# Router on the raw residual, joint placement of both choices, first item by a zero-one product, gate inside the expert results

## The chip, the cores and the metric

The kernel runs on one core of a Trainium2 chip. A core has five engines that run their own instruction streams and meet at semaphores: TensorE (PE, matmuls; weight loads are shown apart as PEld), VectorE (DVE), ScalarE (ACT), GpSimd (POOL) and SyncE (SP, which here only starts transfers). Sixteen DMA engines move data between HBM and the on-chip memory; SP, ACT and POOL each own a queue to them. TensorE's clock has two levels, 2.4 GHz and 1.2 GHz; the profile gives the granted clock of a stretch as 1.00 or 0.50. The metric is the device time of one execution in microseconds (us), the median of several. All data is float32.

## The reference, cut to what matters

Two blocks run one after the other on 512 tokens of 1024 features. The first has two layers of attention, the second one layer of windowed attention beside a convolution, and then the part that this change is about, a mixture of experts:

```python
h2 = rms_norm(x, g_norm2) * (1.0 + sc2) + sh2
x  = x + gt2 * hier_moe(h2, ...)
return rms_norm(x, g_final)

def hier_moe(h, ...):
    g_logits = h @ w_rg + b_rg                       # 4 groups
    grp      = argmax(g_logits)
    e_logits = (h @ w_re + b_re)[token, grp]         # 8 experts of that group
    top_val, top_idx = top_k(e_logits, 2)
    top_w = softmax(top_val) * softmax(g_logits)[grp]
    # each (token, choice) is given to its expert; out = sum of top_w * expert(h)
    expert(x) = (silu(x @ w_gate[e]) * (x @ w_up[e])) @ w_down[e]   # 1024 -> 512 -> 1024
```

There are 32 experts, so 1024 (token, choice) pairs in all. `sc2`, `sh2` and `gt2` are rows of 1024 that come from a condition vector.

## The kernel before

The program is one block of instructions per engine, written out by hand; no scheduler orders it. What sets the order on an engine is the order of the code, and what sets it between engines are semaphores. Tokens lie in four tiles of 128 (`TT = 4`), features in eight blocks of 128 (`KT = 8`). PE writes into eight banks: four that ACT empties (`act_banks`), two for transposes (`tr_banks`, ACT too) and two that DVE empties (`dve_banks`). `claim` takes the next bank of a set and waits until it was freed.

**Before the experts.** `project_out("wout2", ...)` multiplies the mixed rows by the output weights in two halves of four token tiles. DVE adds each half to the residual `x` (`residual_part`, lines 1519 and 1522). When both halves of a tile are in, ACT squares it (line 926), POOL turns the sum into 1/rms in six small instructions (`rstd`, lines 1231 to 1241), DVE scales the tile into `C_tok` (`scale_tile`, line 1429), PE transposes it (`norm_tile`, line 489) and ACT applies scale and shift on the way into `hT` (line 934). Then PE makes the 36 router logits of each tile with 128 tokens stationary and 36 columns moving (line 796).

**Routing.** DVE (`route`) adds the bias (line 1344), picks the group and the two experts (`first_of`, to line 1363), and PE counts how many tokens before each one chose the same expert, by ten products with a matrix of ones and four with a triangular one (lines 805 and 807). DVE then works out the places of the first and of the second choice one after the other (lines 1367 to 1399), which gives `dest`. Each expert owns 96 rows (`SLOTS`); tokens beyond them go to further items.

**Rows and items.** POOL scatters the normed rows from `C_tok` to `expert_rows` in HBM with eight indirect transfers (line 1276), waits for all, and loads 96 rows for the first item and 96 for the second (`load_rows`, line 1281). An item is one expert on 96 rows, in a wide part of 64 and a narrow part of 32: PE transposes its rows (`flip_rows`, line 821), DVE scales and shifts them (`flip`, lines 1861 and 1864), PE multiplies by gate and up weights (`gate_up`, line 831), ACT and DVE make the SwiGLU, PE transposes (lines 855, 860) and multiplies by the down weights (`down`, line 838), ACT copies both results out (lines 1183 and 1185) and issues six stores (line 1190). SP loads the 6 MB of weights of item n+2 into the places that item n frees. 35 items run, the last three for tokens beyond 96 rows.

**Tail.** POOL gathers two result rows for each token, tile by tile (line 1304). Per tile ACT weighs the first (line 1209), DVE adds the weighted second (1901), multiplies by the gate `norm_row` (1902) and adds to `x` (1903), ACT squares (1217). After all four tiles POOL makes four 1/rms columns at once, DVE multiplies four tiles by them and the final gain (line 1908), and SP stores them.

**Two earlier places.** In the second layer's input products DVE forms the modulation rows and runs the 31 taps of the convolution (line 1779), and in front of the first layer's rotary part it forms the columns `mods[3]` and `aff[3]` (scale and shift of the rows for the experts).

## Time and profile before

| | us |
|---|---|
| median of 3 runs | 1803.24 |
| lowest, highest | 1801.92, 1804.38 |
| the profiled execution | 1801.39 |
| its span, first to last instruction | 1799.7 |
| PE busy | 1618.8 (90%) |
| DVE, ACT, POOL busy | 667.6 (37%), 423.0 (24%), 95.9 (5%) |
| mean share of the DMA engines over the span | 391.49 MB, 218 GB/s |

PE is busy nearly everywhere, so the places to read are those where it is not. The page's row of forty slices shows them: the first slice, the slices 24 and 25 (1080 to 1170 us, five tenths busy), and the last one. The first stretch is routing, the last one the tail. Between them stand the experts with PE at nine tenths and the DMA engines at nine tenths too. The chain that ended last is 79% PE, 12% DVE and 4% DMA.

### The profile page before, as it was taken

To read this page: it belongs to the slowest core of one execution; us is meant where nothing else is said; L and a number is where in the kernel's file an instruction comes from. 1 tells how busy PE (TensorE), PEld (TensorE's weight loads), DVE (VectorE), ACT (ScalarE), POOL (GpSimd) and SP (SyncE) were. 2 spreads that over 40 slices of the span, in tenths; PEclk is the share of its full clock that TensorE was granted. 3 is DMA by queue.
4 is the path that set the end of the run, shared out by engine and by line. 5 is a ranking of instruction groups with operands and counts; after the bars stand their busy time and mean duration, and the time that the engine had idled before them with its cause. 6 is when DMAs were issued, how large, how long until landed. Compare 5 with 4: busy or idle time off the path is not lost.

```text
span 1799.7 us, 23161 instructions
## 1 busy us (share of the span) xinstructions
PE 1618.8 (90%) x8968; PEld 810.9 (45%) x8968; DVE 667.6 (37%) x1203; ACT 423.0 (24%) x935; POOL 95.9 (5%) x223
## 2 busy tenths in 40 slices
PE   2999999789899999989998995599999999999990
PEld 2444445554455446546445645244444444444440
DVE  5664006972564133236995424111111111111114
ACT  2433005641201434232005422011111111111112
POOL 3000000111000000020000010200000000000002
PEclk9999999999999999999998995799999999999995
DMA  9653137800675310034220015599999999999974
GB/s 346 227 187 113 47 140 234 275 30 19 221 238 177 140 48 1 13 139 152 94 94 1 1 63 229 202 392 383 403 407 400 409 402 407 404 399 410 398 308 149
DMA packets 112007, 391.49 MB, mean 218 GB/s; under 512 B 11303, under 2 KB 20184, under 8 KB 102600
## 3 DMA queue, kind: packets, MB, share of 16 engines
q1 hardware_dynamic: 84960, 324.02, 47.0%
q0 software_dynamic: 12368, 44.96, 7.7%
q10 hardware_dynamic: 14616, 21.67, 3.4%
q8 instruction: 40, 0.66, 0.1%
q14 instruction: 23, 0.19, 0.0%
HBM read 348.54 MB, written 42.07 MB: 217 GB/s over the span
## 4 chain that ended last, share of the span: by engine, by line
PE 79%; DVE 12%; DMA 4%; ACT 2%; issue 2%; POOL 1%; ACTq 0%; DVEq 0%; SPq 0%; POOLq 0%
PE score_banks L831 20%; PE bank L513 13%; PE bank L838 10%; PE score_banks L505 10%; PE score_banks L513 8%; DVE bufD L1779 4%; PE bank L489 4%; PE score_banks L821 2%; PE bank L724 2%; PE score_banks L660 2%; PE score_banks L717 1%; PE bank L664 1%; DMA slots<-in_w_exp_up 1%; DVE bufD L1444 1%; DMA slots<-in_ada_w 1%
## 5 line engine op out<-in xcount | busy, mean ns | idle before, releaser
L831 PE MATMUL score_banks<-slots,hT 128*32 128x256 f32 (+1 forms) x3360 | 375.5, 453 | 3.7 <-DVE hT L1864 2.3
L831 PEld LDWEIGHTS score_banks<-slots,hT 128*32 128x32 f32 (+1 forms) x3360 | 148.0, 119 | 229.0 <-issue 187.0
L505 PE MATMUL score_banks<-hT,slots 128*128 128x512 f32 (+1 forms) x480 | 201.0, 577 | 11.1 <-ACTq L938 6.1
L838 PE MATMUL bank<-slots,hT 128*32 128x256 f32 (+1 forms) x1680 | 193.1, 454 | 0.0
L513 PE MATMUL score_banks<-slots,hT 128*128 128x512 f32 (+1 forms) x448 | 186.2, 575 | 0.9 <-PE score_banks L505 0.3
L513 PE MATMUL bank<-slots,hT 128*128 128x512 f32 x384 | 167.0, 594 | 2.7 <-ACTq L1007 1.5
L1870 DVE TENSOR_TENSOR mix<-probsT,score_banks 128x256 f32<-128x256 f32 x35 | 14.8, 422 | 382.4 <-ACT probsT L1171 382.4
L505 PEld LDWEIGHTS score_banks<-hT,slots 128*128 128x128 f32 x480 | 93.0, 196 | 113.5 <-issue 104.2
L513 PEld LDWEIGHTS score_banks<-slots,hT 128*128 128x128 f32 x448 | 86.3, 198 | 93.7 <-issue 93.7
L838 PEld LDWEIGHTS bank<-slots,hT 128*32 128x32 f32 (+1 forms) x1680 | 69.9, 118 | 111.4 <-issue 88.4
L513 PEld LDWEIGHTS bank<-slots,hT 128*128 128x128 f32 x384 | 72.2, 190 | 93.5 <-issue 91.5
L1779 DVE SCALAR_TENSOR_TENSOR bufD<-bufC,col,bufD 128x512 f32<-128x512 f32 x120 | 80.5, 748 | 0.5 <-DVE norm_row L1494 0.3
L1171 ACT ACTIVATE probsT<-score_banks 128x256 f32<-128x256 f32 x35 | 13.4, 384 | 276.6 <-PE score_banks L831 276.6
L1444 DVE SCALAR_TENSOR_TENSOR bufD<-slots,silu_c,bufD 128x512 f32<-128x512 f32 x98 | 73.7, 752 | 4.2 <-DVE bufD L1444 0.5
L513 PE MATMUL bank<-slots 128*128 128x512 f32 x160 | 69.7, 593 | 1.3 <-ACTq L1007 1.0
L821 PE MATMUL score_banks<-k_sb,bufD 96*128 96x96 f32 x288 | 37.4, 274 | 30.3 <-DMA bufD<-expert_rows 30.3
L1628 DVE TENSOR_REDUCE negmax<-score_banks 128x2 f32<-128x1024 f32 x32 | 39.0, 1222 | 61.0 <-PE score_banks L660 60.2
L1519 DVE TENSOR_TENSOR mix<-bank,gate_row 128x512 f32<-128x512 f32 x24 | 16.6, 692 | 117.4 <-PE bank L513 117.3
L1444 DVE SCALAR_TENSOR_TENSOR slots<-slots,silu_c 128x512 f32<-128x512 f32 x70 | 52.6, 752 | 11.3 <-DMA slots<-in_w_mod 4.5
L1861 DVE TENSOR_TENSOR hT<-score_banks,aff 128x384 f32<-128x384 f32 x72 | 36.8, 553 | 42.9 <-PE score_banks L821 42.9
L505 PE MATMUL score_banks<-slots 128*128 128x512 f32 x104 | 46.9, 611 | 3.9 <-ACTq L1094 3.3
L1872 DVE TENSOR_TENSOR mix<-probsT,score_banks 128x128 f32<-128x128 f32 x35 | 10.0, 286 | 105.1 <-ACT probsT L1173 105.1
(269 smaller groups left out, 1640.0 us busy)
## 6 DMA issues: line engine op xcount, KB each, us to landing
slots<-in_w_exp_gate SPq DMA_DIRECT2D x35, 2048.0 KB, 16.7
slots<-in_w_exp_up SPq DMA_DIRECT2D x35, 2048.0 KB, 21.4
slots<-in_w_exp_down SPq DMA_DIRECT2D x35, 2048.0 KB, 22.2
slots<-in_w_in SPq DMA_DIRECT2D x16, 2048.0 KB, 8.2
slots<-in_w_mod SPq DMA_DIRECT2D x24, 1024.0 KB, 5.3
slots<-in_ada_w SPq DMA_DIRECT2D x18, 1024.0 KB, 7.3
expert_rows<-norm_row POOLq DMA_DIRECT2D x1, 16896.0 KB, 62.5
bufD<-expert_rows POOLq DMA_DIRECT2D x36, 384.0 KB, 7.2
```

The source lines that it names most:

```text
L489: last = nc.tensor.transpose(bank[:, i * P:(i + 1) * P], piece, ident)
L505: last = mm(bank[:, cols], w[:, k, lo:lo + P], src[:, k, cols], start=(k == 0), stop=(k == kts - 1))
L513: last = mm(bank[:, 0:cols], src[:, k, t * P:(t + 1) * P], rhs(k), start=(k == 0), stop=(k == kts - 1))
L660: return mm(bank[:, :], A8[r, h, t * P:(t + 1) * P], B8[r, h, :], start=True, stop=True)
L724: last = mm(bank[:, c * P:(c + 1) * P], pT[:, j * P:(j + 1) * P], C_tok[:, j, h * P:(h + 1) * P], start=(j == 0), stop=(j == TT - 1))
L821: last = nc.tensor.transpose(psum[k // BANK_K][:, col:col + SLOTS], every_8th(xg[p], k), ident[0:SLOTS, 0:SLOTS])
L831: last = mm(out, xgT[p][:, k, lo:lo + size], e_gu[p][:, :, k, c * cols:(c + 1) * cols], start=(k == 0), stop=(k == KT - 1))
L838: last = mm(bank[c * size:(c + 1) * size, 0:cols], piece, e_down[p][:, f, c * cols:(c + 1) * cols], start=(f == 0), stop=(f == FT - 1))
L1444: return v.scalar_tensor_tensor(out=acc, in0=w, scalar=c, in1=acc, op0=ALU.mult, op1=ALU.add)
L1628: v.tensor_reduce(negmax[:, 2 * i:2 * i + 2], pair, AX.X, ALU.max, negate=True).then_inc(max_ready, 1)
L1779: conv_at[j] = steps(v.scalar_tensor_tensor(out=conv[:, j, :], in0=src, scalar=wcol, in1=conv[:, j, :], op0=ALU.mult, op1=ALU.add))
L1861: v.tensor_tensor(xg_t[:, ks, :], psum[b][:, 0:BANK_K * SLOTS].rearrange("p (k s) -> p k s", k=BANK_K), aff[3][:, ks].unsqueeze(2).to_broa ...
```

## The change

Four things are changed, and a few follow from them.

1. **Router.** The tiles of `x` are transposed as they are (`raw_tile`), without the norm. The router weights are multiplied beforehand by `aff[3]` (`w_scaled`), and the shift's part of the logits is summed on PE into the bias (`w_shift`). The product has the 36 weight columns stationary and 384, then 128 tokens moving; its result is transposed back by four small transposes. DVE multiplies the logits by 1/rms.
2. **Ranks and places.** DVE adds up the masks of the tiles ahead (`above`), PE makes all ranks in one product each with the triangular matrix and the ones, one more for the totals and one for the sums of further items. The places of both choices are worked out in one row of 8 instead of two rows of 4, and the divisions by 96 with a rounding constant instead of a count of comparisons. The order of some small instructions moves.
3. **First item.** DVE builds a zero-one matrix (`onehot`) that says which token sits in which of the first item's 96 rows; PE multiplies the normed rows by it (`pick_rows`, 32 products) instead of waiting for scatter and load. POOL's load of item 0 is left out.
4. **Gate and tail.** The two results of an item are multiplied by the gate on their way out of PSUM by DVE (`gated_results`), no longer copied by ACT, which only issues the stores. In the tail DVE adds both gathered rows to `x` with their weights, and the last norm runs tile by tile.

```diff
+            def raw_tile(t):
+                pe.wait_ge(x_ready, 12 + t + 1)
+                for k in range(0, KT, 4):
+                    transposes(tr_banks, tr_filled, [every_8th(x[:, t, :], k + j) for j in range(4)])
-            project_out("wout2", hT, 2, lambda: out2(TT - 1), lambda t: norm_tile(3, t, every_8th), ((0,), (1, 2)))
+            project_out("wout2", hT, 2, lambda: out2(TT - 1), raw_tile, {2: (0,), 3: (1,), 4: (2, 3)})
...
-                for k in range(KT):
-                    last = mm(bank[:, t * R:(t + 1) * R], hT[:, k, t * P:(t + 1) * P], w_router[:, k, :],
+            for lo, hi in ((0, TT - 1), (TT - 1, TT)):
+                hT_of(3, hi - 1)
+                bank = act_banks.claim(pe)
+                cols = slice(lo * P, hi * P)
+                for k in range(KT):
+                    last = mm(bank[0:R, cols], w_scaled[:, k, :], hT[:, k, cols], start=(k == 0), stop=(k == KT - 1))
...
+            mm(bank[:, 0:n], upper, flat(mask_v), start=True, stop=False)
+            pe.wait_ge(mask_ready, 2)
+            mm(bank[:, 0:n], ones, flat(above[:, 0:TT, :]), start=False, stop=True)
+            mm(bank[0:EXPERTS, n + EXPERTS:n + EXPERTS + 1], above[:, TT, :], ones[:, 0:1], start=True, stop=True).then_inc(dve_filled, 1)
+            pe.wait_ge(further_ready, 1)
+            bank = dve_banks.claim(pe)
+            mm(bank[:, 0:EXPERTS + 1], ones[0:EXPERTS, :], further_sum[0:EXPERTS, :], start=True, stop=True).then_inc(dve_filled, 1)
...
+            def pick_rows():
+                pe.wait_ge(xn_ready, 4 * TT)
+                pe.wait_ge(onehot_ready, 1)
+                for k in range(KT):
+                    col = k % BANK_K * SLOTS
+                    for t in range(TT):
+                        last = mm(psum[k // BANK_K][:, col:col + SLOTS], every_8th(C_tok[:, t, :], k), onehot[:, t, :],
+                                  start=(t == 0), stop=(t == TT - 1))
+                last.then_inc(xg_read, 1)
-            flip_rows(0, 16, 0, first=True)
+            pick_rows()
...
+                for k, hot in enumerate((onehot, onehot_2)):
+                    steps(v.tensor_tensor(hot, slot_ids.unsqueeze(1).to_broadcast([P, TT, SLOTS]),
+                                          place[:, k * TT:(k + 1) * TT].unsqueeze(2).to_broadcast([P, TT, SLOTS]), ALU.is_equal))
+                steps.settle()
+                chain(v.tensor_tensor(onehot, onehot, onehot_2, ALU.add))
+                dve.sem_inc(onehot_ready, 1)
...
+            chain(v.tensor_tensor(w_scaled[:, :, :], w_router[:, :, :], mods[3][:, 0:8].unsqueeze(2).to_broadcast([P, KT, R]), ALU.mult))
+            chain(v.tensor_reduce(w_shift[:, :], w_scaled[:, :, :].rearrange("p k n -> p n k"), AX.X, ALU.add))
+            dve.sem_inc(w_shift_ready, 1)
+            chain(v.tensor_tensor(w_scaled[:, :, :], w_router[:, :, :], aff[3][:, :].unsqueeze(2).to_broadcast([P, KT, R]), ALU.mult))
...
+            bank = dve_banks.take(dve)
+            v.tensor_tensor(b_router[:, :], b_router[:, :], bank[:, 0:R], ALU.add).then_inc(dve_freed, 1)
...
+            def gated_results(p, n, stores=None):
+                dve.wait_ge(down_done, 2 * n + 1)
+                if stores is not None:
+                    dve.wait_ge(y_out[p], 16 * Y_STORES * stores)
+                v.tensor_tensor(y_wide[p], psum[6][:, :], gate_wide, ALU.mult).then_inc(y_ready, 1)
+                dve.wait_ge(down_done, 2 * n + 2)
+                v.tensor_tensor(y_narrow[p], psum[7][:, 0:256], gate_narrow, ALU.mult).then_inc(y_ready, 1)
...
                 swiglu(0, 2 * i)
                 flip(1, 2 * i + 1)
+                gated_results(0, 2 * i, i)
...
+            add_results(0)
+            add_results(1)
+            dve.wait_ge(norm_row_in, 32)
+            last_norm(0)
+            add_results(2)
+            last_norm(1)
+            add_results(3)
+            last_norm(2)
+            last_norm(3)
```

PE from the output projection to the first item, before. `w_router` is the router's weights, `bufC` the normed rows, `bufE` holds the masks, `bufD` the loaded rows of an item, `slots` all large weights:

```order
L489 MATMUL bank<-k_sb,bufC 128x128 x8
L513 MATMUL bank<-slots,hT 128x512 x8
L489 MATMUL bank<-k_sb,bufC 128x128 x16
L796 MATMUL bank<-w_router,hT 128x36 x16
L489 MATMUL bank<-k_sb,bufC 128x128 x8
L796 MATMUL bank<-w_router,hT 128x36 x16
...
L805 MATMUL bank<-bufE,k_sb 128x32 x4
L821 MATMUL score_banks<-k_sb,bufD 128x96 x8
L831 MATMUL score_banks<-slots,hT 64x512 x16
```

The same place of the changed kernel; line 501 is the transposing helper, 816 the router's product, 857 `pick_rows`:

```order
L501 MATMUL bank<-k_sb,x 128x128 x8
L525 MATMUL bank<-slots,hT 128x512 x8
L501 MATMUL bank<-k_sb,x 128x128 x8
L525 MATMUL bank<-slots,hT 128x512 x8
L501 MATMUL bank<-k_sb,x 128x128 x16
L816 MATMUL score_banks<-hT,w_router_scaled 36x384 x8
L816 MATMUL score_banks<-hT,w_router_scaled 36x128 x8
L821 MATMUL bank<-k_sb,mix 128x36 x4
L827 MATMUL bank<-bufE,k_sb 128x128
L829 MATMUL bank<-bufE,k_sb 128x128
...
L857 MATMUL score_banks<-probs,bufC 128x96 x32
L867 MATMUL score_banks<-slots,hT 64x512 x16
```

Two transposed tiles now stand ahead of the last tile of the projection where one stood, two behind it, and no router product waits between transposes.

DVE in the tail, before (the last two of four tiles, and the last norm):

```order
L1901 SCALAR_TENSOR_TENSOR slots<-slots,wts 128x1024 [waits dve_step,first_results_weighted,results_gathered3]
L1902 TENSOR_TENSOR slots<-slots,norm_row 128x1024 [waits dve_step]
L1903 TENSOR_TENSOR x<-x,slots 128x1024 [waits dve_step]
L1908 SCALAR_TENSOR_TENSOR slots<-x,ss,gate_row 128x1024 [waits dve_step,norm_row_loaded,rstd_ready]
L1908 SCALAR_TENSOR_TENSOR slots<-x,ss,gate_row 128x1024 x3
```

and from the second tile on in the changed kernel:

```order
L1978 SCALAR_TENSOR_TENSOR x<-slots,wts,x 128x1024 [waits dve_step,results_gathered1]
L1978 SCALAR_TENSOR_TENSOR x<-slots,wts,x 128x1024 [waits dve_step]
L1984 SCALAR_TENSOR_TENSOR slots<-x,ss,gate_row 128x1024 [waits dve_step,rstd_ready,norm_row_loaded]
L1978 SCALAR_TENSOR_TENSOR x<-slots,wts,x 128x1024 [waits results_gathered2]
L1978 SCALAR_TENSOR_TENSOR x<-slots,wts,x 128x1024 [waits dve_step]
L1984 SCALAR_TENSOR_TENSOR slots<-x,ss,gate_row 128x1024 [waits dve_step,rstd_ready]
```

Each tile has two instructions instead of three ahead of its norm, and the norm of tile 0 to 2 (line 1984, waiting on POOL) stands between the additions of later tiles.

## Rows read from the trace of the kernel before

**Rows 1.** Windows: engines' busy us (and instructions), granted clock, DMA share, GB/s.
```profile
1098.00:1146.00 48.00, 8.22 (x39) 7.69 (x41) 21.46 (x96) 1.70 (x3) 9.60 (x11) 0.50 0.43 162
1146.00:1690.00 544.00, 543.78 (x4819) 230.26 (x4817) 83.36 (x155) 71.45 (x186) 15.72 (x31) 1.00 0.99 391
```
**Rows 2.** Timeline of PE, routing: start, length, instruction, count, idle before and its releaser.
```profile
1069.14 7.03 PE L513 MATMUL bank<-slots,hT 128*128 128x512 f32 x16
...
1091.33 6.88 PE L796 MATMUL bank<-w_router,hT 128*128 128x36 f32 x32
...
1141.90 1.52 PE L821 MATMUL score_banks<-k_sb,bufD 96*128 96x96 f32 x8 [30.32 <-DMA bufD<-expert_rows]
1145.69 12.47 PE L831 MATMUL score_banks<-slots,hT 128*64 128x512 f32 x96 [2.27 <-DVE hT L1864]
```
**Rows 3.** Timeline of DVE, routing.
```profile
1076.94 0.69 DVE L1522 TENSOR_TENSOR x<-x,mix 128x512 f32<-128x512 f32 x1
...
1098.25 0.31 DVE L1344 TENSOR_TENSOR bufE<-bank,b_router 128x144 f32<-128x144 f32 x1 [16.59 <-PE bank L796]
...
1100.13 0.87 DVE L1355 TENSOR_TENSOR bufE<-bufE 128x32 f32<-128x32 f32 x4
...
1105.00 0.29 DVE L1363 TENSOR_TENSOR bufE<-bufE 128x128 f32<-128x128 f32 x1
...
1111.62 0.33 DVE L1367 COPY bufE<-bank 128x160 f32<-128x160 f32 x1 [6.02 <-PE bank L805]
...
1123.19 0.17 DVE L1399 CAST dest<-bufE 128x4 int32<-128x4 f32 x1
1123.51 0.49 DVE L1402 TENSOR_TENSOR bufE<-bufE,k_sb 128x320 f32<-128x320 f32 x1
```
**Rows 4.** Timeline of POOL, scatter and first loads.
```profile
1123.72 1.29 POOL L1276 DMA_INDIRECT expert_rows<-bufC,dest  x1 [42.84 <-DVEq L1400]
...
1137.90 1.11 POOL L1281 DMA_DIRECT2D bufD<-expert_rows  x2 [4.07 <-DMA expert_rows<-bufC,dest]
```
**Rows 5.** Windows around routing, columns as in rows 1: the granted clock beside PE's work.
```profile
1083.00:1090.00 7.00, 7.00 (x35) 7.00 (x35) 0.00 (x0) 2.15 (x6) 0.00 (x0) 0.50 1.03 396
...
1146.00:1150.00 4.00, 4.00 (x12) 1.23 (x10) 0.00 (x0) 0.00 (x0) 0.00 (x0) 0.58 0.23 79
```
**Rows 6.** Chain of work: sixteen narrow PE instructions at full clock.
```profile
1008.58 1.73 PE bank L779 x16
```
**Rows 7.** Timeline of ACT: a copy out of a PE bank.
```profile
935.47 0.60 ACT L1142 ACTIVATE bufE<-score_banks 128x512 f32<-128x512 f32 x1 [6.81 <-PE score_banks L513]
```
**Rows 8.** Timeline of DVE ahead of the first rotary part of the second layer.
```profile
582.84 0.69 DVE L1508 TENSOR_TENSOR mix<-probs,cosT 128x512 f32<-128x512 f32 x1 [7.23 <-ACT probs L918]
```
**Rows 9.** Timeline of PE at the end of the convolution.
```profile
936.34 1.09 PE L489 MATMUL bank<-k_sb,bufD 128*128 128x128 f32 x8 [0.91 <-DVEq L1808]
```
**Rows 10.** DMA issues: direction, count, size, us from issue to landing.
```profile
slots<-in_w_exp_up SPq DMA_DIRECT2D x35, 2048.0 KB, 21.4
```
**Rows 11.** Timeline of all engines in the tail.
```profile
1758.49 3.22 ACTq L1190 DMA_DIRECT2D expert_results<-bufD  x6
1763.84 1.02 POOL L1304 DMA_INDIRECT slots<-expert_results,dest  x1 [45.74 <-DMA expert_results<-bufD]
...
1771.67 1.29 DVE L1901 SCALAR_TENSOR_TENSOR slots<-slots,wts 128x1024 f32<-128x1024 f32 x1 [16.74 <-ACT slots L1209]
...
1773.71 1.15 ACT L1209 ACTIVATE slots<-slots,wts 128x1024 f32<-128x1024 f32 x1 [2.15 <-DMA slots<-expert_results,dest]
...
1791.41 4.87 DVE L1908 SCALAR_TENSOR_TENSOR slots<-x,ss,gate_row 128x1024 f32<-128x1024 f32 x4 [3.83 <-POOL ss L1241]
```
**Rows 12.** Timeline of POOL in an earlier norm.
```profile
787.68 0.19 POOL L1239 TENSOR_SCALAR pw<-pw 128x1 f32<-128x1 f32 x1
...
788.23 1.29 POOL L1231 TENSOR_SCALAR pw<-ss 128x1 f32<-128x1 f32 x1
```
**Rows 13.** Timeline of DVE at the same moment.
```profile
788.18 1.28 DVE L1433 SCALAR_TENSOR_TENSOR x<-x,ss,norm_row 128x1024 f32<-128x1024 f32 x1 [1.81 <-POOL ss L1241]
```

More of the change, by code:

```diff
@@ L748, in _ @@
                     reduce_row()
+            pe.wait_ge(w_shift_ready, 1)
+            bank = dve_banks.claim(pe)
+            mm(bank[:, 0:R], ones, w_shift[:, :], start=True, stop=True).then_inc(dve_filled, 1)
             close_unit(dve_filled, dve_banks)
@@ L1165, in _, with item @@
             fn(rt_d, rt_d, ACT.Exp).then_inc(gexp_out, 1)
-            def item(p, n, stores, first=False):
+            def item(p, n, first=False):
                 act.wait_ge(gu_done, 2 * n + 1)
@@ new lines, in route @@
+                v.tensor_tensor(rt_d, m2, m1, ALU.subtract).then_inc(gexp_in, 1)
+                both = lambda row: row.unsqueeze(1).to_broadcast([P, 2 * TT, NE])
+                ranks = dve_banks.take(dve)
+                n = TT * NE
+                more = further[0:NE, 0:1]
+                rounded_down(more, ranks[0:NE, n + NE:n + NE + 1], SLOTS / 2 + 0.5)
+                chain(v.tensor_scalar(further_sum[0:NE, :], k_sb[0:NE, K_UPPER:K_UPPER + NE + 1], more, None, ALU.mult))
+                dve.sem_inc(further_ready, 1)
@@ new lines, in route @@
+                for k in range(2):
+                    steps(v.tensor_tensor(picked[:, k * TT:(k + 1) * TT, :], hots[:, k * TT:(k + 1) * TT, :],
+                                          ranks[:, 0:n].rearrange("p (t e) -> p t e", t=TT), ALU.mult))
+                steps.settle()
+                dve.sem_inc(dve_freed, 1)
+                chain(v.tensor_reduce(rank, picked, AX.X, ALU.add))
+                rounded_down(ones_of, rank, SLOTS / 2 - 0.5)
+                chain(v.scalar_tensor_tensor(out=slot, in0=ones_of, scalar=-float(SLOTS), in1=rank, op0=ALU.mult, op1=ALU.add))
@@ L1400, in route @@
-                dve.sem_inc(dest_ready, 1)
-                chain(v.tensor_tensor(item_cmp, incl.unsqueeze(1).to_broadcast([P, OVER, NE]),
+                chain(v.tensor_tensor(picked, hots, both(before[:, 0:NE]), ALU.mult))
+                chain(v.tensor_reduce(over, picked, AX.X, ALU.add))
+                chain(v.scalar_tensor_tensor(out=over, in0=ones_of, scalar=float(NE - 1 - BEYOND), in1=over, op0=ALU.add, op1=ALU.add))
+                chain(v.tensor_tensor(over, over, firsts, ALU.subtract))
@@ new lines, in route @@
+                chain(v.scalar_tensor_tensor(out=over, in0=ones_of, scalar=1.0, in1=over, op0=ALU.min, op1=ALU.mult))
+                chain(v.tensor_tensor(over, over, firsts, ALU.add))
+                chain(v.scalar_tensor_tensor(out=place, in0=over, scalar=float(SLOTS), in1=slot, op0=ALU.mult, op1=ALU.add))
+                chain(v.tensor_scalar(place, place, float(SLOTS * BEYOND), None, ALU.add))
+                chain(v.tensor_copy(dest[:, :, :].rearrange("p k t -> p (k t)"), place))
+                dve.sem_inc(dest_ready, 1)
```

229 lines of the change are left out of this document (116 added, 113 removed).

## The prediction

> **What bounds the kernel now.** I read the page's row of forty slices first, since PE's busy share alone (90%) hides where it waits, then windows, then timelines of single engines. In the expert loop PE works 543.78 of 544 us [rows 1]: nothing taken from ACT or DVE there shortens it. Routing is different: from 1098 to 1146 us PE works 8.22 of 48 us at half clock and DVE 21.46 [rows 1]. It is a chain of single engines: the last output product ends at 1076.2 [rows 2], the logits reach DVE at 1098.25, the masks are done at 1105.3, DVE waits 6.02 us for the ranks and starts at 1111.62, `dest` is done at 1123.4 [rows 3], POOL starts at 1123.72 and the rows load from 1137.90 [rows 4], PE transposes at 1141.90 and the first item starts at 1145.69 [rows 2]. That is 69.5 us from output product to item, and everything in it is on the path. The tail is the second such chain, from the stores at 1758.49 over gathers and DVE to the last norm, which ends at 1796.3 [rows 11], 3.4 us ahead of the span's end.
>
> **Router.** The order now lets PE transpose raw tiles as soon as DVE has added them. One transposed tile more ahead of the last output product, about 1.1 us (eight transposes, from 1.09 in [rows 9]), puts its end at 77.4 (I leave out 1000 from here on). DVE adds for 0.69 us twice [rows 3], so x is there at 78.9. Eight transposes end at 80.0, and ACT, already idle for them, ends its second copy (0.60 each [rows 7]) at 80.9. The 384-column product is eight matmuls, in the trace sixteen instructions: 16 instructions of 512 columns take 7.03 at full clock [rows 2], so 384 take 5.2; for 128 columns 1.8. They run from 80.0 to 87.0. ACT's copy, four transposes and two hand-overs: 0.8. DVE starts the logits at 87.8, not 98.25: **10.4 us**. The norm runs beside it: ACT's square of tile 3 starts at 80.9, square and POOL's six instructions took 3.83 in the tail for four columns [rows 11], `scale_tile` at most the 1.22 of a norm there (4.87 for four), so it ends by 86.0 and hides.
> Whether the clock holds is open: in before it was at half from 1083 to 1090, behind the gap that follows the last output product, and stayed so through 7.00 us of unbroken work [rows 5]. In the new order PE waits there for about 0.5 us, so I take full clock. At half clock the two products take 7.0 more.
>
> **Masks and ranks.** From logits to masks before: 7.05 us [rows 3]. Chained instructions cost their length plus about 0.035: small ones 0.20, 128 elements 0.32, 256 about 0.45, 320 0.52 [rows 3]. Added: one of 144 (0.34). Gone: three index corrections (0.61), three of the four group maskings (0.58) and a subtraction that moves behind (0.09). That gives 6.1: **0.9 us**. Then 0.85 us for four small sums of 32, and PE's last two products with their latency 0.9 (the wait before was 6.02 for 28 instructions): ranks 1.75 after the masks, not 6.3: **4.6 us**.
>
> **Places.** Before: 11.8 us from ranks to `dest` [rows 3]. After, in order: four instructions on the totals 0.85, two products 0.65, a sum over 256 0.45, three roundings 0.63, slot 0.20, copy 0.23, product and sum 0.90, seven of 8 elements 1.41. Together 5.35: **6.4 us**. PE's product of the further items runs beside the roundings. `dest` is ready at 1100.95.
>
> **First item.** Before: `dest` to first gate product 22.3 us. After: two comparisons of 384 and their sum, 0.59 each at the slope above, 1.8 in all; 32 products of 96 columns, 64 instructions; 0.15 latency; then the same 2.27 of DVE [rows 2]. A PE instruction with 128 weight columns and few moving takes 0.108 at full clock [rows 6] and 0.215 at half (6.88 for 32 [rows 2]): the products cost 6.9 to 13.8. The clock is at half when they start, since PE has mostly waited since 87. Rows 5 show both courses: the 7.00 us without a rise, and the first gate products, in which it rose about 3.7 us after their start at 1145.69 (0.58 over 1146 to 1150). I take the second, 3.7 us at half and the rest at full, because these are ordinary products of full weights back to back: 8.9. Sum 13.1, a gain of **9.2 us**. Then the first item runs at full clock from its start, which saves 0.42 x 4 = **1.7 us** [rows 5]. Staying at half costs 4.9 + 1.7 = 6.6.
> The Trainium skill ("TensorE: Matmul & The Clock Gate", part 1) says that sustained PE activity releases the throttle. By it the router's products in before should have risen too; the 7.00 us at half clock in rows 5 do not agree, so I don't lean on it and keep the other course as rival A.
> What this uncovers: the second item's rows. Scatter and load still take 18.2 us from `dest` [rows 2, 4], so they land at 1119.2; PE asks for them after the gate products of item 0, at about 1125. The weights of items 0 and 1: the DMA engines are busy for 0.43 of the 48 us behind 1098, 20.6 us [rows 1]; eight scatters of 0.5 MB and two loads of 0.4 at 396 GB/s [rows 5] are 12 of these, so the weights had landed by about 1107, and item 0 now starts at 1114. Both hide, the rows with 6 us to spare. Six small copies of the gate lie beside the first gate products.
>
> **Expert loop.** DVE gets two multiplications of about 0.7 and 0.4 us per item, of 15 us in which it is idle (83.36 busy in 544 [rows 1]). PE needs the banks back only at the next item's down product. I cost this at nothing. ACT starts the wide stores somewhat earlier.
>
> **Tail.** The last item's narrow stores no longer stand behind two wide ones: six issues took 3.22 [rows 11], four take 2.2, less the slightly slower multiplication: 0.8. First rows are weighed by DVE, not ACT: 1.2 sooner. Gathers land tile after tile about 3 us apart [rows 11], so DVE adds tile 0 and 1 until 1775.5 and then alternates. What sets the rest is POOL. Six instructions make a column, in at most 2.6 us if alone (3.83 less a square of 1.2, for four columns); but in the one place where such an instruction ran beside DVE's two-operand instruction it took 1.29 instead of 0.19, until DVE had ended [rows 12, 13]. DVE is busy without a break in the new tail, so three of the six wait for one DVE instruction each. Stepping through it gives norms of tiles 0 to 3 at 1776.8, 1781.6, 1786.4 and 1789.5, the last ended at 1790.7, and 3.1 us of store: 1793.8, not 1799.7: **5.9 us**. Without any such wait it is 8.5; if DVE waits in turn, 3.1.
> The Trainium skill ("SBUF — State Buffer", on the shared port pair) calls this an exclusive lock that either side holds for a whole instruction. The rows agree for POOL's side (1.29 against 0.19); that DVE waits too no row here shows, and by it the tail would gain the 3.1.
>
> **Earlier costs.** Three instructions on 288 elements (1.5 us) ahead of the rotary part have 7.23 us of idle DVE [rows 8]. In the convolution DVE is the bound (PE waits 0.91 for it [rows 9]), and one bank of bias costs **-0.35**. Fifty more kilobytes of constants at the start: 0.1, dropped.
>
> **Sum.** 10.4 + 0.9 + 4.6 + 6.4 + 9.2 + 1.7 + 5.9 - 0.35 = 38.7 us. The profiled execution took 1801.39 (span 1799.7), so 1762.7 for one like it. The median of the three runs lies 1.85 above that execution, hence **1764.5**.
>
> **Rivals.** *A, the narrow products stay at half clock* (first item 13.8): 32.1 gained, 1771.1. For it: the first row of rows 5. Against: the second row of rows 5. *B, the router's product runs at half clock too*: 7.0 less again, 1778.1 with A, 1771.5 without. For it: the half clock at 1083; against: the gap ahead of it is gone. *C, the tail is free of POOL's waits*: 2.6 more, 1761.9, and 1.8 us better still if the first item's products rise at once. *D, slower than before*: the loop turns from PE-bound to DMA-bound. 155 DVE instructions, five for an item, are 31 items of 17.5 us in 544 [rows 1]. Up weights land 21.4 us after issue [rows 10], which stands behind item n's gate products; item n+2 needs them 24.3 after these (17.5, and 17.5 less 10.7). That is under 3 us of slack, and the DMA engines are at 0.99 [rows 1]. If stores issued earlier push the landing by more than that, every item grows by what is over; from 1.2 us over (33 items, 39 us) the whole gain is gone, at 2 us over the time is 1830. Against: the bytes per item are the same. *E, the second item's rows become the bound*: POOL issues the scatters while DVE works on; if that doubled their 14.2 us, the rows would land at 1133 and item 1 would wait 8 us: 1772.5. Against: in before POOL issued one in 1.29 us beside DVE's work [rows 4].
>
> **Chances.** The forecast 50%, A 23%, B 8%, C 12%, D 2%, E 3%, and 2% within the noise. The range from 1759 to 1776 takes in C, A and B without A and leaves out the rest. Faster by over 0.2% (3.6 us, about what a measurement of this kernel can tell from no change) 96%, within it 2%, slower 2%.
>
> **What would show it.** In the changed kernel's timeline DVE's first router instruction should stand about 9 to 11 us behind the last output product; ranks 1.8 after the masks; 64 instructions of `pick_rows` in 9 us, with a granted clock that rises inside them; the first gate product at about 1114, its 96 instructions in 10.7 us; items 17.4 us apart as before; POOL's small instructions in the tail up to 1.3 us long. A first item later than 1122, items further apart than 17.5, or a tail as long as before would prove it wrong.

## The result and the profile after

The changed kernel takes 1773.47 us (median of four runs, 1771.25 to 1776.98), the kernel before 1802.58 in the same session: a ratio of 0.9835, 95% interval 0.982 to 0.9849, so 29.1 us less. The forecast was 1764.5, in a range of 1759 to 1776: direction and range held, the size came out 9 us short. The profiled execution spans 1769.1 us, where the one of before spans 1799.7. All medians here are of runs in the chip's faster state, so one run each of two variants below, `packed_tail` (3075 us) and `busy_tail` (5710 us), is not in theirs.

The windows over the same stretches as [rows 1], columns as there: the stretch from 1098 to 1146 us is now mostly PE's work, and the loop behind it is as full as it was.

```profile
1098.00:1146.00 48.00, 40.65 (x245) 25.42 (x247) 14.95 (x45) 1.32 (x4) 9.92 (x11) 0.71 0.66 250
1146.00:1690.00 544.00, 544.00 (x4871) 231.00 (x4871) 118.48 (x218) 41.41 (x125) 15.72 (x31) 1.00 1.02 402
```

PE's timeline of the routing, the counterpart of [rows 2]: router product, four transposes of logits, the rows product (L857), the first item's gate and up products (L867), the second item's.

```profile
1079.72 7.10 PE L816 MATMUL score_banks<-hT,w_router_scaled 128*36 128x384 f32 x32
1086.74 0.72 PE L821 MATMUL bank<-k_sb,mix 36*128 36x36 f32 x4
...
1103.07 15.52 PE L857 MATMUL score_banks<-probs,bufC 128*128 128x96 f32 x64 [5.80 <-DVEq L1444]
1120.87 13.12 PE L867 MATMUL score_banks<-slots,hT 128*64 128x512 f32 x96 [2.27 <-DVE hT L1916]
...
1140.71 1.51 PE L867 MATMUL score_banks<-slots,hT 128*64 128x512 f32 x6
```

DVE's timeline, the counterpart of [rows 3]: logits, the last mask, the totals as soon as the ranks are there, `dest`, and the zero-one matrix.

```profile
1087.51 0.31 DVE L1388 TENSOR_TENSOR bufE<-bank,ss 128x144 f32<-128x144 f32 x1 [2.95 <-PE bank L821]
...
1093.33 0.29 DVE L1402 TENSOR_TENSOR bufE<-bufE 128x128 f32<-128x128 f32 x1
...
1095.77 0.14 DVE L1372 TENSOR_SCALAR bufE<-bank 32x1 f32<-32x1 f32 x1 [0.74 <-PE bank L830]
...
1100.93 0.17 DVE L1437 CAST dest<-bufE 128x8 int32<-128x8 f32 x1
1101.25 1.03 DVE L1440 TENSOR_TENSOR probs<-k_sb,bufE 128x384 f32<-128x384 f32 x2
1102.31 0.56 DVE L1443 TENSOR_TENSOR probs<-probs 128x384 f32<-128x384 f32 x1
```

Everything up to the rows product stands within 0.4 us of where the forecast put it. Then the product takes 15.52 us, not 8.9, and the first item's gate products 13.12, not 10.7. The first item still starts 24.8 us sooner than in before (1120.87 against 1145.69).

The tail, the counterpart of [rows 11]: first gather, DVE's weighting of tile 0, POOL's power instruction beside it, and the four last norms (L1984) with what DVE waited for.

```profile
1737.03 1.01 POOL L1339 DMA_INDIRECT slots<-expert_results,dest  x1 [43.83 <-DMA expert_results<-bufD]
...
1743.52 2.61 DVE L1978 SCALAR_TENSOR_TENSOR x<-slots,wts,x 128x1024 f32<-128x1024 f32 x2 [10.56 <-DMA slots<-expert_results,dest]
...
1747.88 1.62 POOL L1269 TENSOR_TENSOR pw<-pw,half_neg 128x1 f32<-128x1 f32 x1
...
1750.72 1.28 DVE L1984 SCALAR_TENSOR_TENSOR slots<-x,ss,gate_row 128x1024 f32<-128x1024 f32 x1 [1.65 <-POOL ss L1277]
...
1755.16 1.29 DVE L1984 SCALAR_TENSOR_TENSOR slots<-x,ss,gate_row 128x1024 f32<-128x1024 f32 x1 [0.64 <-POOL ss L1277]
...
1759.87 1.28 DVE L1984 SCALAR_TENSOR_TENSOR slots<-x,ss,gate_row 128x1024 f32<-128x1024 f32 x1 [0.91 <-POOL ss L1277]
...
1762.97 1.29 DVE L1984 SCALAR_TENSOR_TENSOR slots<-x,ss,gate_row 128x1024 f32<-128x1024 f32 x1 [1.81 <-POOL ss L1277]
```

And the closing instructions of the program (those of its last line: engine queue, instruction, length in ns, start): SyncE, which waits for the last store, is through at 1767.1, POOL only at 1762.7 + 6.2 = 1768.9.

```profile
L136 POOLq DRAIN  x1: 6212/6212/6212, 1762.7 to 1762.7; - x1
...
L136 SPq DRAIN  x1: 13/13/13, 1767.1 to 1767.1; - x1
```

### The profile page after: what moved, and what is told of

It is laid out like the page before. It is cut to its first block, busy times and chain, and to the rows that moved or that the text cites. A ratio compares the mean times of both kernels' runs of the same rounds, so it can differ in the third digit from the quotient of the medians.

```text
span 1769.1 us, 23135 instructions
## 1 busy us (share of the span) xinstructions
PE 1623.6 (92%) x8978; PEld 810.3 (46%) x8978; DVE 701.8 (40%) x1251; ACT 377.5 (21%) x839; POOL 107.0 (6%) x240
## 4 chain that ended last, share of the span: by engine, by line
PE 82%; DVE 11%; DMA 2%; ACT 2%; issue 1%; POOL 1%; ACTq 0%; DVEq 0%; SPq 0%; POOLq 0%
PE score_banks L867 21%; PE bank L525 13%; PE bank L874 11%; PE score_banks L517 10%; PE score_banks L525 8%; DVE bufD L1828 4%; PE bank L501 4%; PE score_banks L846 2%; PE bank L736 2%; PE score_banks L672 2%; PE score_banks L729 1%; PE bank L676 1%; DVE bufD L1489 1%; DMA slots<-in_ada_w 1%; DMA slots<-in_w_mod 1%
## 5 line engine op out<-in xcount | busy, mean ns | idle before, releaser
L867 PE MATMUL score_banks<-slots,hT 128*32 128x256 f32 (+1 forms) x3360 | 376.2, 454 | 2.3 <-DVE hT L1916 2.3
L867 PEld LDWEIGHTS score_banks<-slots,hT 128*32 128x32 f32 (+1 forms) x3360 | 147.5, 119 | 228.5 <-issue 186.4
L1267 POOL TENSOR_SCALAR pw<-ss 128x1 f32<-128x1 f32 (+2 forms) x27 | 8.4, 311 | 766.6 <-ACT bufC L962 440.4
L1317 POOL DMA_DIRECT2D bufD<-expert_rows x35 | 17.8, 509 | 563.5 <-PE score_banks L846 556.6
## 6 DMA issues: line engine op xcount, KB each, us to landing
slots<-in_w_exp_up SPq DMA_DIRECT2D x35, 2048.0 KB, 20.7
```

Source lines behind the costliest of these rows:

```text
L867: last = mm(out, xgT[p][:, k, lo:lo + size], e_gu[p][:, :, k, c * cols:(c + 1) * cols], start=(k == 0), stop=(k == KT - 1))
```

## The experiments

Two questions were open: why the rows product took 15.5 us, and why the tail gave less than forecast. Executions of one and the same instruction sequence reach the routing up to 6.8 us apart (the transposes behind the last output product start at 1076.48 in `pool_late` and at 1083.25 in `tail_act`, two variants that differ from the changed kernel only later, and at 1077.19 in the changed kernel itself). A median of a few runs therefore carries some microseconds of chance, and I compare traces by the distance from these transposes to the first item's gate products: 69.2 us before (1076.48 to 1145.69), 43.7 after.

### Is it the clock? Work for PE ahead of the rows product

`late3` and `both6` give PE filler products of 512 columns, whose results nobody uses, in its pauses. `late3` has three ahead of the rows product, `both6` six there and six beside the masks. The edit of `late3`:

```diff
+            def keep_busy(n):
+                for _ in range(n):
+                    mm(psum[2], ident, C_tok[:, 0, 0:W], start=True, stop=True)
...
             pe.wait_ge(dve_freed, dve_banks.n)
+            keep_busy(3)
```

> The changed kernel, with three more products of 512 columns (results not used) on PE in the gap of 5.7 us between the product of the counts of further items and the first item's rows. Theory (the rows product was slow because PE had been nearly idle since 1086.8 and the clock had fallen to 0.50): the work in the gap brings the clock back near the rows product, which then takes 8 to 10 us instead of 15.5 with a granted clock of 1.00 for most of it; with the first item's gate product at 10.7 instead of 13.1 the whole is 1764 to 1768. Rival 1 (narrow products stay at the half clock whatever ran before): clock 0.50 in them, 15.5 us, 1773.5. Rival 2 (clock returns, but the 2.3 us pause of PE for the flip on DVE takes it away again): rows 8 to 10 us, gate product still 13.1, about 1767.

> The changed kernel, with six more products of 512 columns (results not used) on PE while DVE forms the masks (gap 1087.5 to 1093.6) and six more in the gap before the rows product, so that PE works nearly without pause from Wout2 on. Theory (the clock falls because PE stands): granted clock 1.00 throughout 1076:1120, the two rank products 0.4 us each instead of 0.8, rows product 7.8 us, first gate product 10.7 us: 7.7 + 2.4 + 0.8 = 10.9 us less, 1762.6. Rival 1 (narrow products lose the clock by themselves): full until 1103 and then 0.50, rows product 12 to 15.5 us, 1769 to 1773. Rival 2 (the extra products overrun the masks): the rank products start later than 1093.7 by up to 1 us and the gain is that much smaller.

Measured: `late3` 1773.95 us, `both6` 1777.05. No gain in either. The distance is 44.2 and 46.5 us: in `both6` the products before the rows product overran (7.66 us from 1099.54, since they stood behind PE's wait for its banks). The rival that expected no change had the right time and the wrong reason. The clock did come back, and the rows product did not get shorter. Windows of `late3` (columns as in [rows 1]; an instruction is counted in every window that it touches, so neighbouring windows count some twice):

```profile
1108.00:1110.00 2.00, 2.00 (x10) 2.00 (x10) 1.02 (x6) 0.00 (x0) 1.39 (x3) 1.00 1.03 414
1110.00:1112.00 2.00, 2.00 (x10) 2.00 (x10) 0.00 (x0) 0.00 (x0) 1.70 (x2) 1.00 1.03 414
1112.00:1114.00 2.00, 2.00 (x10) 2.00 (x10) 0.00 (x0) 0.00 (x0) 1.39 (x3) 0.74 1.02 418
1114.00:1116.00 2.00, 2.00 (x10) 2.00 (x9) 0.00 (x0) 0.00 (x0) 0.66 (x1) 0.50 1.04 424
```

A window of 2 us touches ten instructions at a granted clock of 1.00 (2.4 GHz) and ten at 0.50 (1.2 GHz): the pace is the same. The product took 15.31 us, 0.24 for each of its 64 instructions. PE was busy without a pause throughout, and the clock fell inside it. My theory for the 15.5 us, and my forecast's choice between 8.9 and 13.8, both rested on the clock. That theory fell.

### Is it how the weights are read?

`straight` takes 128 neighbouring columns as the stationary operand, and so computes other columns for the first item's rows:

```diff
-                        last = mm(psum[k // BANK_K][:, col:col + SLOTS], every_8th(C_tok[:, t, :], k), onehot[:, t, :],
+                        last = mm(psum[k // BANK_K][:, col:col + SLOTS], C_tok[:, t, k * P:(k + 1) * P], onehot[:, t, :],
```

> The changed kernel, with the rows product reading 128 neighbouring columns of the token rows as its stationary operand instead of every eighth (it computes other columns for the first item's rows: that part of the computation is changed). Theory (the stride costs in the weight load, 0.2425 us for an instruction here against 0.215 in the transposes at the same clock): 13.8 us instead of 15.5. Rival (the fp32 weight load takes this long with any stride): 15.5 us.

Measured: 1765.87 us (one run), product 10.01 us, distance 38.2. The weight loads of the product, length in ns (least, median, most), in the changed kernel, in `late3` and in `straight`:

```profile
L857 PEld LDWEIGHTS score_banks<-probs,bufC x64: 312/334/340, 1103.0 to 1118.0; 128*128 128x128 f32 x64
```
```profile
L865 PEld LDWEIGHTS score_banks<-probs,bufC x64: 313/334/338, 1106.1 to 1121.3; 128*128 128x128 f32 x64
```
```profile
L857 PEld LDWEIGHTS score_banks<-probs,bufC x64: 192/192/333, 1103.9 to 1113.6; 128*128 128x128 f32 x64
```

With every eighth column a load takes 334 ns at either clock. With neighbouring columns it takes 333 at half clock and 192 at full, and the clock comes back within the product. I had expected 13.8 us, from the stride's cost at half clock alone; the clock's return brought the rest. So narrow products do not stay at half clock, as rival A had it: in `straight` (columns as above) the clock is back by 1110.

```profile
1106.00:1108.00 2.00, 2.00 (x11) 2.00 (x11) 1.04 (x7) 0.00 (x0) 1.40 (x2) 0.50 1.04 416
1108.00:1110.00 2.00, 2.00 (x14) 2.00 (x13) 0.00 (x0) 0.00 (x0) 1.69 (x2) 0.63 1.00 404
1110.00:1112.00 2.00, 2.00 (x21) 2.00 (x20) 0.00 (x0) 0.00 (x0) 1.39 (x3) 1.00 1.02 418
```

`strides` then lets the stride grow inside one product (1, 2, 4, 8, sixteen instructions each; it too computes other columns):

```diff
+                                  C_tok[:, t, 0:P << k // 2].rearrange("p (q k) -> p k q", k=1 << k // 2)[:, 0, :], onehot[:, t, :],
```

> The changed kernel with PE kept at work by products whose results are not used (six beside the masks, three before the rows product, so that the clock is 1.00 when it starts), and with the stationary operand of the rows product read with a column stride that grows: 1 for the first two feature blocks (16 instructions), then 2, 4 and 8 (it computes other columns for the first item's rows: that part of the computation is changed). Theory 1 (any stride over 1 is slow): 0.115 us an instruction in the first 1.8 us, 0.24 us in all the rest, weight loads of 192 and of 334 ns, about 13.4 us in all. Theory 2 (the cost grows with the stride): 0.115, then steps up to 0.24 only at stride 8, about 10 to 11 us. Rival (the slow read belongs to the tile or to the scatter's reads beside it, not to the stride): no step within the product.

Measured: 1769.33 us (one run), with the filler products in it. Windows of the weight loads (busy us and count, granted clock, DMA share, GB/s; the product runs from 1104.52 for 11.49 us):

```profile
1105.00:1106.00 1.00, 1.00 (x11) 1.00 1.01 406
1106.00:1107.00 1.00, 1.00 (x11) 1.00 1.02 406
1107.00:1108.00 1.00, 1.00 (x10) 1.00 1.04 422
1108.00:1109.00 1.00, 1.00 (x7) 1.00 1.03 410
1109.00:1110.00 1.00, 1.00 (x5) 1.00 1.03 410
1110.00:1111.00 1.00, 1.00 (x6) 1.00 1.01 414
...
1114.00:1115.00 1.00, 1.00 (x6) 0.50 1.04 426
```

Neither theory had it: there is one step, and it stands between stride 2 and stride 4. Thirty-two instructions at 0.115 us and thirty-two at 0.24 make 11.4, and 11.49 was measured; the rate changes after 1108, with the clock still at 1.00. The Trainium skill ("SBUF — State Buffer", the note on cachelines) says that a read wants at least two accesses in a line of 16 bytes for full bandwidth. The step agrees: stride 2 of fp32 has two in a line, stride 4 one. The same note lets one stride over 4 fp32 values at no cost; that this run does not bear out. Nor is the line the whole story: the transposes of x read with a stride of 8 and load at full pace (last section).

### What the zero-one product is worth against a load

`loaded_rows` undoes the third part: `load_rows(0, 0)` is back on POOL, `flip_rows(0, 16, 0, first=True)` on PE, and the zero-one matrix is gone.

> The changed kernel with the first item's rows loaded from the scattered rows as before, and without the zero-one matrix. Theory (at the half clock the zero-one product is worth little): from the places to the first gate product 22.4 us as before, instead of 19.8 now, so slower by 2.6 us: 1776. Rival (the part is worth what was forecast, since what was lost at the half clock is lost elsewhere too): slower by 9 us, 1782.5. Rival 2: rows would have come in time now that the scatter starts earlier: 0.

Measured: 1778.44 us, distance 48.1, so 4.4 us longer than after (5.0 by the medians), between the 2.6 and the 9 that were expected. From the first scatter to the gate products it takes 23.8 us, in before 22.0: the scatters now start 22 us earlier, while the DMA engines still bring the first items' weights (share 1.03 from 1104 to 1112, and in before 0.56 from 1124 to 1128 and 0.93 to 1132), and POOL waits longer for the rows to have left. In `loaded_rows`:

```profile
1110.83 0.95 POOL L1312 DMA_INDIRECT expert_rows<-bufC,dest  x1 [0.30 <-issue]
1117.58 1.10 POOL L1317 DMA_DIRECT2D bufD<-expert_rows  x2 [5.80 <-DMA expert_rows<-bufC,dest]
```

The same wait is 4.07 us in [rows 4]. That the busier DMA engines cause the longer wait is inferred from these shares; no run separates it.

### A version without the stride, and one that holds the clock

`packed` lets ACT, idle beside the masks, copy the token rows into `hT` in the order that the product reads. `packed_busy` adds PE's filler products, now ahead of the wait for its banks.

```diff
+            act.wait_ge(xn_ready, 4 * TT)
+            for t in range(TT):
+                fn(packed[:, t], C_tok[:, t, :].rearrange("p (q k) -> p k q", k=KT), ACT.Copy).then_inc(packed_ready, 1)
...
-                        last = mm(psum[k // BANK_K][:, col:col + SLOTS], every_8th(C_tok[:, t, :], k), onehot[:, t, :],
+                        last = mm(psum[k // BANK_K][:, col:col + SLOTS], packed[:, t, k, :], onehot[:, t, :],
```

> The changed kernel, with the token rows copied once more by ACT (4 copies of 1024 columns, beside the masks on DVE) into the transposed-tile buffer in the order that the rows product reads, so that its stationary operand is 128 neighbouring columns; nothing else differs and the outputs are the reference's. Theory (every eighth column holds the weight load of a two-instruction fp32 product at 334 ns whatever the clock; neighbouring columns let it follow the clock): rows product 9.5 to 10.5 us instead of 15.5, clock back at 1.00 within it, first gate product 12.4 instead of 13.1, together 6 us less: 1767.5. Rival (the run with other columns was lucky in its upstream part; the copy on ACT is late or costs as much as it saves): rows product starts after 1103.1 or keeps 15 us, 1771 to 1775.

> The kernel with the packed rows, and the products of 512 columns (results not used) that keep PE at work: six beside the masks, three after the counts of further items, these before PE waits for its banks so that they end by 1103. Theory (without the stride the rows product follows the clock, and the clock stays up while PE works): rows product 7.8 to 8.5 us, gate product 10.7 to 12.4, 2 to 3.5 us less than the packed kernel alone: 1764 to 1765.5. Rival (the pauses of 0.5 to 1.7 us between the rank products lose the clock anyway): rows product 9 to 10 us, no gain over packed.

Measured: `packed` 1765.89 us (ratio to before 0.9789, 0.977 to 0.9807), product 10.75 us, distance 38.9; against `loaded_rows` (48.1) the zero-one product is then worth 9.2 us. `packed_busy` 1766.3 (0.9778 to 0.9809), product 7.36 at a granted clock of 1.00, first gate products 12.38, distance 35.2. By the trace the second is 3.7 us better than the first, by five timed runs each there is nothing between them; that pair alone leaves it unclear. The pause between the two products is a cost of its own. In `packed_busy` the clock is still at 1.00 when the rows product ends, PE then waits 2.27 us for DVE, and 1.3 us into the gate products the clock falls:

```profile
1102.01 7.36 PE L868 MATMUL score_banks<-probs,hT 128*128 128x96 f32 x64 [1.58 <-DVEq L1458]
1111.64 12.38 PE L878 MATMUL score_banks<-slots,hT 128*64 128x512 f32 x96 [2.27 <-DVE hT L1930]
```
```profile
1112.00:1113.00 1.00, 1.00 (x8) 0.39 (x6) 0.91 (x4) 0.00 (x0) 0.00 (x0) 0.99 1.02 418
1113.00:1114.00 1.00, 1.00 (x6) 0.45 (x4) 0.51 (x2) 0.00 (x0) 0.00 (x0) 0.50 1.03 422
```

The four copies on ACT took 7.86 us in all and ended at 1097.3, well before the product:

```profile
1089.47 7.86 ACT L1219 ACTIVATE hT<-bufC 128x1024 f32<-128x1024 f32 x4
```

### The tail

`tail_act` takes the four reciprocal roots off POOL; `pool_late` puts four zero fills behind them; `tail_before` undoes the fourth part.

```diff
-                fn(bufC[:, t * D:(t + 1) * D], x[:, t, :], ACT.Square, accum_out=ss[:, t:t + 1]).then_inc(squares_ready, 1)
+                steps(fn(bufC[:, t * D:(t + 1) * D], x[:, t, :], ACT.Square, accum_out=ss[:, t:t + 1]))
+                steps.settle()
+                fn(ss[:, t:t + 1], ss[:, t:t + 1], ACT.Sqrt, bias=tiny[:, 8:9], scale=1.0 / D).then_inc(rstd_ready, 1)
...
-            tile_rstds(0, 1, 2, 3)
...
                 wait_rstd()
+                chain(v.reciprocal(ss[:, t:t + 1], ss[:, t:t + 1]))
```

> The changed kernel, with the four reciprocal roots of the last norm taken off POOL: ACT takes the square root behind each sum of squares and DVE the reciprocal. Theory (two things end the program late: DVE's waits of 1.65, 0.91 and 1.81 us for POOL, and POOL's closing drain of 6.2 us that starts at its last instruction): last norm ends 3 to 3.5 us earlier, POOL's drain ends by 1753, the last store ends the span, 5 us less in all: 1768.5. Rival 1 (the drain does not matter, the end is tied to the last store): 3.3 less, 1770. Rival 2 (the root needs a table on ACT that is loaded each time between squares): DVE waits for ACT as long as for POOL before, only the 2 us of the drain are gained, 1771.5.

> The changed kernel with four zero fills of 512 columns added on POOL behind its last reciprocal root; nobody waits for them. Theory (POOL's closing drain of 6.2 us sets the end of the program): the drain starts behind the fills and the span is longer by their whole time, read from the trace (some 1 to 4 us). Rival (the drain is there but the last store's landing sets the end, or the drain is shorter when it starts later): the distance from the last store's landing to the end stays 2.0 us.

> The changed kernel with its fourth part undone: results copied out of PSUM by ACT without the gate, in the tail a weighting on ACT and three operations of DVE for each tile, one reciprocal root for all four tiles. Theory (the loop is bound by PE and doesn't feel who empties the banks, the tail gained 4.8 us): items 17.40 us apart, 54 + 4.8 = 58.9 us from the last item's gate products to the end, 1778.3. Rival (the gate's product on DVE costs in the loop and the part is worth less): items closer than 17.40 us, less than 4 us slower.

Measured: `tail_act` 1769.17 us. From the first gather to the end 26.9 us (1743.20 to 1770.1) against 32.1 after (1737.03 to 1769.1). DVE waits for no root longer than 0.22 us, POOL's drain is over at 1746.3 + 14.7 = 1761.0, and the last store ends the program 3.05 us behind the last norm (1767.05), where after takes 4.84 (1764.26 to 1769.1). So of the 5.2 us, 3.4 come from DVE's waits for the roots and 1.8 from the end.

```profile
1764.32 1.28 DVE L1987 SCALAR_TENSOR_TENSOR slots<-x,ss,gate_row 128x1024 f32<-128x1024 f32 x1
1765.57 0.16 DVE L1986 RECIPROCAL ss<-ss 128x1 f32<-128x1 f32 x1
1765.77 1.28 DVE L1987 SCALAR_TENSOR_TENSOR slots<-x,ss,gate_row 128x1024 f32<-128x1024 f32 x1
```
```profile
L136 POOLq DRAIN  x1: 14703/14703/14703, 1746.3 to 1746.3; - x1
```

The root's table was loaded once on ACT, 1.28 us, and DVE did not wait for it. `pool_late` shows the drain by itself. The fills run for 1.92 us from 1763.23, and the end moves from 2.0 us behind SyncE's last step to 3.9:

```profile
L136 POOLq DRAIN  x1: 8042/8042/8042, 1763.1 to 1763.1; - x1
...
L136 SPq DRAIN  x1: 13/13/13, 1767.4 to 1767.4; - x1
...
L136 SPq EVENT_SEMAPHORE  x1: 17/17/17, 1771.3 to 1771.3; - x1
```

Its median, 1773.8 us, is only 0.3 above that of the changed kernel, whose own runs spread over 5.7 us, so here the trace decides and the medians don't.

`tail_before` took 1776.9 us. From the last item's gate products to the end it takes 58.7 us (1716.14 to 1774.8), before 58.9 (1740.80 to 1799.7), after 54.1 (1715.00 to 1769.1). From the first item's start to the last's it takes 594.1 us both in it and after: the loop doesn't feel who empties the banks. By these traces the part is worth 4.6 us, all of it in the tail (3.4 by the medians).

### Together

`packed_tail` joins `packed` and `tail_act`; `busy_tail` adds the filler products, two of them after the rows product.

```diff
             pick_rows()
+            keep_busy(2)
             item(0, 16, 0, first=True, ahead=lambda: flip_rows(1, 16, 1))
```

> The kernel with the packed rows (about 6 us from the rows product on) and the roots of the last norm on ACT and DVE (about 4.3 us at the end): the two lie at different ends of the program and should add up, 1773.5 - 7.6 - 4.3 = 1761.6. Rival (the tail's gain was a matter of which run is compared): 1765.

> The same, with the products of 512 columns (results not used) that keep PE at work: six beside the masks, three before the rows product, two in the pause of 2.3 us between the rows product and the first item. Theory (the first item's gate product was at 12.4 us since the clock fell in that pause): granted clock 1.00 from 1076 to the first item's end, rows product 7.4 us, gate product 10.7 us; against the kernel before it in this list 3.5 us less for the rows product and the ranks, and 1.7 for the gate product: 1756.5. Rival (as the timed runs of the two kernels with packed rows say, which differ by 0.4 us where their traces differ by 3.7: what is won there is lost behind it): within 1 us of the kernel before it in this list.

Measured: `packed_tail` 1762.7 us (ratio 0.9771, 0.9745 to 0.9797), `busy_tail` **1758.18** (0.9745, 0.972 to 0.9769), 15 us below the changed kernel and the fastest here. The distances are 38.2 and 35.2 us. PE in `busy_tail`:

```profile
1105.01 7.36 PE L868 MATMUL score_banks<-probs,hT 128*128 128x96 f32 x64 [1.61 <-DVEq L1461]
1112.20 1.91 PE L823 MATMUL score_banks<-bufC,k_sb 128*128 128x512 f32 x4
1114.64 10.68 PE L878 MATMUL score_banks<-slots,hT 128*64 128x512 f32 x96 [0.53 <-DVE hT L1933]
```

Product at full clock, no pause of 2.3 us behind it, gate products at 10.68 us like those of any later item. Here medians (4.5 us apart) and traces (3.0 up to the gate products and 1.7 in them) agree, though the runs of the two overlap (1757.65 to 1765.18, and 1754.03 to 1760.23). `packed_tail` missed its 1761.6 by 1.1, `busy_tail` its 1756.5 by 1.7.

## Why the prediction held where it did, and where it failed

- **What bounds the kernel**: right. Only the two chains outside the loop moved; items are 17.4 us apart in both.
- **Router**: right. DVE has the logits at 1087.51 (forecast 1087.8), and the product ran at full clock, 7.10 us for 7.0. Rival B did not come.
- **Masks, ranks, places**: right within 0.4 us. The masks end at 1093.62, the ranks are there 2.15 us behind (1.75 forecast), `dest` is written at 1101.1 (1100.95).
- **First item**: the step that failed. The term was 9.2 us and came to 2.5. I priced the 64 instructions at 0.108 to 0.215 us from [rows 2, 6], rows of products whose stationary operand is 128 neighbouring columns. This one reads every eighth column, and so costs 0.2425 at either clock (15.52 in all). The diff said `every_8th`; I did not ask what it does to the load. The "3.7 us at half and the rest at full" then failed as a result: at this pace the clock did not rise, and in `late3` it fell. `straight`, `strides` and `packed` show it from three sides. A smaller part of the same term was wrong as well: even with neighbouring columns the product took 10.0 to 10.8 us and not 8.9, for the clock rose 5.6 us (`straight`) to 7.1 us (`packed`) behind its start and not 3.7.
- **First item at full clock**: a second failure, of the path behind the product: -0.65 instead of 1.7 (13.12 against 12.47 before). The sum carries PE's 2.27 us of waiting for DVE between rows and gate products, but takes it that the clock holds across them. `packed_busy` shows that it doesn't: it leaves the rows product at 1.00 and its gate products still take 12.38 us. With filler products in the pause (`busy_tail`) they take 10.68. Without them they took 12.0 to 13.6 in every run, whether the rows product read with a stride or not. So mending the read alone does not win the 1.7 us: in the changed kernel the clock is at 0.50 before the pause begins, and where it isn't, the pause brings it down.
- **Rival A** named nearly the time (1771.1) with a mechanism that `straight` refutes. It held 23% for a reason that wasn't there. That the measured time lies inside my range is luck in part: the range reached up to 1776 to take in this rival and B, not for a slow read.
- **The second item's rows**: right, hidden; they land at about 1123 (1119.2 forecast), and PE transposes them at 1134.20 without a wait. E did not come, nor D: up weights land 20.7 us after issue (21.4 in [rows 10]), the DMA share is 1.02.
- **Tail**: mechanism right, size 4.8 for 5.9. POOL's instructions are stretched beside DVE as forecast (the power instruction 1.62 beside DVE, 0.55 alone; [rows 12]), and DVE's last norm ends 0.6 us sooner than the stepping said (1764.26; the forecast's 1790.7 less the 25.8 that the last item had gained by then). What was missing is the program's end: POOL's drain of 6.2 us outlasts the last store by 2.0 (`tail_act`, `pool_late`). In before it is over at 1797.4, ahead of the last store at 1799.4, so no row of before shows it as a cost:

```profile
L134 POOLq DRAIN  x1: 6303/6303/6303, 1791.1 to 1791.1; - x1
...
L134 SPq DRAIN  x1: 13/13/13, 1799.4 to 1799.4; - x1
```

- **Earlier costs**: the 0.35 us for the bias is too small to be told from the spread of 6.8 us ahead of the routing; no run isolates it.
- **Slips in the working**: the store at the end is put at 3.1 us, but the rows give 3.4 from the last norm to the span's end, so the tail's own sum is 5.6 and not 5.9. 3.7 us at half and the rest at full make 8.8 and not 8.9. And rival E's 1772.5 lies inside the range, though the text leaves it out.
- **Not in the sum**: about 1.6 us more in the last items. Before, the last four start 17.6 to 18.2 us apart instead of 17.4, the last one after a wait of 0.72 us for its up weights; after, they keep to 17.5. `late3` and `loaded_rows` had such waits of 0.5 and 1.6 us, so this comes and goes with the run; it wasn't tested further.

Against the forecast: 6.6 us from the rows product, 2.4 from the gate products (the term's 1.7 and the 0.65 that they took longer than before) and 1.1 from the tail, less 1.6 in the last items, are 8.5 of the 9.0 us that the median lies above it.

## What to carry to other kernels

A price per instruction belongs to its access pattern too: before pricing a product from a row, compare the stride of its stationary operand with that row's, and look for an idle engine that can lay it out side by side beforehand. A clock that stays low can be the result of slow instructions and not their cause; a run that lifts the clock without changing the instructions tells them apart. A wait of PE between two products costs more than its length if the clock falls behind it: 2.3 us of waiting cost 1.7 more here. Look at what every engine does after its last instruction: an engine that finishes late with small work can end the program behind the last store.

## What was new about the hardware

- The weight load of an fp32 product (two instructions per product) of 128 columns takes 192 ns at full and 333 at half clock with neighbouring columns, and 334 at either clock with a stride of 8; a stride of 2 runs at the pace of neighbouring ones (0.115 us an instruction), a stride of 4 at that of 8 (0.24). Single-instruction fp32 transposes of x with a stride of 8 loaded in 194 ns at full clock all the same (16 loads at 1077 to 1080). Why the stride doesn't hurt them was not tried.
- ACT feels the stride too: its copies of 1024 columns in `packed` took 1.97 us each, its weighting of 1024 neighbouring columns, a copy with a scale, 1.15 ([rows 11]).
- The granted clock fell from 1.00 to 0.50 at 1113 in `late3` inside a product that kept PE busy without a pause, and stayed at 1.00 through the same product with packed operands (`busy_tail`, `packed_busy`). It fell in the same way in `both6`, at 1111.
- POOL's closing drain ended 6.0 us after its last instruction had been done where that was arithmetic or a fill (after, `pool_late`), and 7.9 us where it was a gather (`tail_act`).
- In the tail POOL's instructions were stretched beside DVE's (1.62 against 0.55 us), DVE's beside POOL's were not: 2.60 us for two in the changed kernel and in `tail_act`, where POOL is idle. The Trainium skill ("SBUF — State Buffer", on the shared port pair) calls the lock exclusive from either side; for DVE's side no run here shows it.
